# The last two experts' rows kept on chip and added by 0/1 products, pair rows added by GpSimd and TensorE by turns

## What is computed

```python
gate = (softmax(top_v) * pg[:, None])              # two gates a token
h = silu(xb @ w_g[e]) * (xb @ w_u[e])              # D=1024 -> 512
y = (h @ w_d[e]) * wts[:, None]                    # 512 -> 1024
out = zeros_like(xt).at[buf_tok].add(y)            # two rows a token are added
x = layer_norm(ALPHA * x + out, ln3_g, ln3_b)      # ALPHA = 2 ** 0.25
```

## Time and profile before

| | |
|---|---|
| median of 3 runs | 1626.03 us |
| the profiled execution's own time | 1628.42 us |
| its span | 1625.8 us |
| mean granted TensorE clock | 0.978 of full |
| TensorE busy | 1552.3 us (95%) |
| VectorE busy | 1005.0 us (62%) |
| ScalarE busy | 787.0 us (48%) |
| GpSimd busy | 362.8 us (22%) |
| DMA | 352.69 MB, 217 GB/s mean |

### The profile page before, as it was taken

The page is one execution under the profiler, slowest core; times in us unless marked ns, Lnnn a source line. Parts: engine busy times, 40 slices in busy tenths (PEclk is TensorE's granted clock), DMA queues, the critical chain, the costliest instruction groups (busy, mean ns, idle before and its releaser), DMA issues.

```text
span 1625.8 us, 21437 instructions
## 1 busy us (share of the span) xinstructions
PE 1552.3 (95%) x8440; PEld 1279.9 (79%) x8440; DVE 1005.0 (62%) x1282; ACT 787.0 (48%) x1143; POOL 362.8 (22%) x277
## 2 busy tenths in 40 slices
PE   8999999999988999999999988999999999999966
PEld 6877887677766888999777777888888888888842
DVE  5611111777644655222555458989889998999936
ACT  5411121555454013222422234887888887888834
POOL 0000000477862851000122111131111121111005
PEclk9999999999999999999999977999999999999987
DMA  9721111600333545000445536999999999999876
GB/s 356 260 76 39 43 56 59 174 23 19 118 104 132 184 170 193 27 21 1 156 156 175 175 130 251 385 368 396 387 382 399 398 389 393 385 392 398 342 283 282
DMA packets 86331, 352.69 MB, mean 217 GB/s; under 512 B 23512, under 2 KB 28248, under 8 KB 64474
## 3 DMA queue, kind: packets, MB, share of 16 engines
q1 hardware_dynamic: 76106, 331.41, 54.1%
q0 software_dynamic: 9216, 18.89, 3.0%
q10 hardware_dynamic: 912, 1.05, 0.2%
HBM read 321.93 MB, written 43.15 MB: 225 GB/s over the span
## 4 chain that ended last, share of the span: by engine, by line
PE 85%; DVE 5%; DMA 4%; ACT 3%; issue 1%; POOL 0%; SPq 0%; DVEq 0%; POOLq 0%; ACTq 0%
PE M L1348 23%; PE M L1067 12%; PE T L862 6%; PE M L835 6%; PE T L1348 5%; PE T L771 3%; DMA beside<-in_w_exp_up 3%; DVE rounded L1905 3%; PE M L771 3%; PE M L950 2%; PE T L1409 2%; PE T L1139 2%; PE T L1137 2%; PE T L1138 2%; PE M L1171 2%; PE M L1153 2%
## 5 line engine op out<-in xcount | busy, mean ns | idle before, releaser
L1905 DVE TENSOR_TENSOR rounded<-beside,rounded 128x1024 fp32r<-128x1024 f32 (+1 forms) x397 | 471.4, 1233 | 57.2 <-ACT rounded L1791 46.7
L1348 PE MATMUL M<-rounded 128*128 128x512 f32 x1908 | 461.3, 392 | 2.8 <-ACT rounded L1826 1.9
L1348 PEld LDWEIGHTS M<-rounded 128*128 128x128 f32 x1908 | 355.8, 188 | 77.7 <-ACT rounded L1826 2.1
L1791 ACT CAST rounded<-beside 128x1024 fp32r<-128x1024 f32 x256 | 258.9, 1050 | 80.9 <-DMA beside<-in_w_exp_up 75.4
L1067 PE MATMUL M<-rounded 128*128 128x512 f32 x816 | 196.7, 395 | 2.9 <-ACT rounded L1661 1.7
L1067 PEld LDWEIGHTS M<-rounded 128*128 128x128 f32 x816 | 150.1, 188 | 33.9 <-issue 2.0
L1801 ACT CAST rounded<-beside 128x1024 fp32r<-128x1024 f32 x128 | 125.2, 1049 | 24.2 <-DMA beside<-in_w_exp_down 22.3
L2573 POOL DMA_INDIRECT expert_rows<-beside,route_out x32 | 41.8, 1305 | 394.8 <-ACT beside L1832 389.5
L2506 POOL TENSOR_SCALAR arena<-arena,rinv 128x384 f32<-128x384 f32 (+7 forms) x64 | 110.2, 1726 | 48.9 <-DVE rinv L2033 48.7
L1348 PE MATMUL T<-rounded 128*128 128x512 f32 x384 | 108.7, 398 | 0.0
L1905 DVE TENSOR_TENSOR rounded<-T,rounded 128x512 fp32r<-128x512 f32 (+2 forms) x84 | 79.0, 944 | 20.7 <-ACT rounded L1674 17.7
(11 more groups left out here) (374 smaller groups left out, 2462.4 us busy)
## 6 DMA issues: line engine op xcount, KB each, us to landing
beside<-in_w_exp_gate SPq DMA_DIRECT2D x64, 1024.0 KB, 8.1
beside<-in_w_exp_up SPq DMA_DIRECT2D x64, 1024.0 KB, 10.9
beside<-in_w_exp_down SPq DMA_DIRECT2D x32, 2048.0 KB, 11.4
arena<-x_rows SPq DMA_DIRECT2D x27, 512.0 KB, 3.7
x_rows<-arena SPq DMA_DIRECT2D x18, 512.0 KB, 3.1
arena<-expert_rows SPq DMA_DIRECT2D x9, 1024.0 KB, 12.7
arena<-in_x_prompt SPq DMA_DIRECT2D x16, 512.0 KB, 3.9
arena<-in_cache_mem_k SPq DMA_DIRECT2D x8, 1024.0 KB, 5.7
```

Source lines behind the costliest of these rows:

```text
L1348: got = nc.tensor.matmul(out, x[xs], (high, low)[ws](w)[:, c:c + 512], start=(first and n == 0), stop=(last and n == 2))
L1791: nc.scalar.copy(as_both(high(c)), both_raw(c)).then_inc(gu_high, 1)
L1905: return nc.vector.tensor_tensor(out, x, highs.bitcast(f32), ALU.subtract)
```

## The change

1. **Gates in the expert rows.** VectorE computes the gates (divided by ALPHA) before it goes on with the split, multiplies the one-hot matrices `r_hot` with them, and TensorE brings them to slots: 18 plain float32 matmuls of 128x32, ahead of expert 0's transposes. The 20 idle-filling matmuls become 6. `slot_gate` holds a gate for each slot of each expert; ScalarE multiplies by it where it copied before (`results`).
2. **The last two experts stay on chip.** Rows of experts 30 and 31 aren't scattered. ScalarE and VectorE write them as high and low parts over `xT_parts`. GpSimd makes 18 0/1 matrices `hots` (slot by token, one for each expert and tile) in block 28, and TensorE adds the rows by products with them: two parts by two halves, for each expert and tile. The DRAM rows that are never written must read as zero, so SP zeroes all of `expert_rows` (9.4 MB) early.
3. **Pair rows.** Tiles 1, 3, 5 and 7 are added by TensorE with the identity in plain float32 (`pair_rows`), tiles 0, 2, 4, 6 and 8 by GpSimd, two additions a tile (`add_pairs`). VectorE adds `T` to every tile.
4. **Loads.** The x2 rows are loaded in the raw weights' place during the last block, the pair rows while expert 31's gate/up product frees its chunks, once the scatters of experts 28 and 29 have landed.
5. **Last down products.** Expert 31's hidden rows are turned between chunks 1 and 2 of expert 30's down product (`last_two_down`), and the splits on ScalarE and VectorE are reordered to match.
6. **Finish.** Tiles go in the order 0 to 8. Six of them (all but 4, 5 and 6) are finished on VectorE with PSUM operands.

The diff, cut to its core:

```diff
@@ SP, early and in the last block
+            sp.dma_start(ye_dram.rearrange("(p a) (h c) -> p (a h) c", p=P, c=CW),
+                         conv_w[:, 2, :].unsqueeze(1).to_broadcast([P, 4 * NT, CW])).then_inc(pairs_zeroed, 16)
...
+                        for g in (0, 1):
+                            sp.wait_ge(gu_low, 8 * b + 4 * (g + 1))
+                            for t in range(4 * g, 4 * g + 4):
+                                load_x2(t)
...
+            def load_pairs(t):
+                if t < PT:
+                    sp.wait_ge(gu_used, 8 * more + 8 * (NE - 1) + t + 1)
+                else:
+                    sp.wait_ge(down_low, 4 * more + 4 * NE)
+                sp.dma_start(yk[t], ye_pairs[t * P:(t + 1) * P, :, :]).then_inc(last_in[t], 16)
...
-            sp.wait_ge(ye_out[1], 16 * (NE // 2))
-            sp.wait_ge(ye_out[0], 16 * more + 16 * (NE // 2))
+            sp.wait_ge(ye_out[0], 16 * (NE // 2 - 1))
+            load_x2(PT)
+            sp.wait_ge(ye_out[1], 16 * (NE // 2 - 1))
@@ TensorE, before the experts
-            for _ in range(20):
+            for _ in range(6):
                 nc.tensor.matmul(M[0][:, 0:512], sel_slot[:, 0, 0, :], sel_slot[:, 0, 0:4, :], start=True, stop=True)
+            pe.wait_ge(sel_ready, 3)
+            for k in (0, 1):
+                for t in range(NT):
+                    to_slots = sel_slot[:, k, t, :] if t < PT else sel_last[:, k, 0, :]
+                    got = nc.tensor.matmul(T[1][:, 0:NE], to_slots.bitcast(f32), r_hot[:, k, t, :], ...)
+            got.then_inc(rank_ps, 1)
@@ TensorE, the last two experts
+            def last_two_down(b):
+                pe.wait_ge(hidT_high, b)
+                pe.wait_ge(hidT_low, b)
+                pe.wait_ge(ye_rows, b - 1)
+                for k in range(4):
+                    pe.wait_ge(down_low, 4 * b - 4 + k + 1)
+                    x = [hidT_parts[1 - b % 2][s][:, k * P:(k + 1) * P] for s in (0, 1)]
+                    for c in (0, 512):
+                        got = split_product(M[1][:, c:c + 512], x, 8 + k, c, k == 0, k == 3)
+                    got.then_inc(down_used, 1)
+                    if k == 1:
+                        turn_hidden(b, b % 2)
+                last_down(b, b % 2)
@@ TensorE, the finish
+            def rows_of_last(e, t):
+                for part in (0, 1):
+                    for c in (0, 512):
+                        got = nc.tensor.matmul(T[t % 2][:, c:c + 512], hots[e][t], xT_parts[e][part][:, c:c + 512], ...)
+                return got
+
+            def pair_rows(t):
+                pe.wait_ge(last_in[t], ROWS_IN[t])
+                for k in (0, 1):
+                    for c in (0, 512):
+                        nc.tensor.matmul(T[t % 2][:, c:c + 512], ident, yk[t][:, k, c:c + 512], start=(k == 0), stop=False)
@@ ScalarE
-                nc.scalar.copy(yo[u], M[1][:, :]).then_inc(ye_rows, 1)
+                nc.scalar.mul(yo[u], M[1][:, :], gate).then_inc(ye_rows, 1)
...
-                split_down(b, range(4))
+                split_down(b, (0, 1))
                 if not coming:
                     hidden_high(b, u)
+                split_down(b, (2, 3))
@@ VectorE, the finish
+            for p in range(NT):
+                if p - 1 in BY_GAIN:
+                    shift_of(p - 1)
+                if p == PT:
+                    add_shift(p - 2)
+                sum_rows(p)
+                if 0 < p < PT and p - 1 not in BY_GAIN:
+                    scale_shift(p - 1)
+                if p < PT and p - 2 in BY_GAIN:
+                    add_shift(p - 2)
+                if p not in BY_GAIN:
+                    centre_gain(p)
                 add_eps(p)
@@ GpSimd, the finish
+            def add_pairs(t):
+                pool.wait_ge(last_in[t], ROWS_IN[t])
+                nc.gpsimd.tensor_tensor(xl[t], xl[t], yk[t][:, 0, :], ALU.add).then_inc(pool_step, step.next())
+                pool.wait_ge(pool_step, step.value())
+                nc.gpsimd.tensor_tensor(xl[t], xl[t], yk[t][:, 1, :], ALU.add).then_inc(pairs_added, 1)
...
+            add_pairs(BY_POOL[0])
+            for n, t in enumerate(BY_POOL[1:]):
+                add_pairs(t)
+                inverse_deviation(n)
```

More of the change, by code:

```diff
@@ L115, in sem @@
             return ctx.enter_context(nc.semaphore(name))
+        with nc.sbuf_tensor("ident_only", [P, P], f32), nc.sbuf_tensor("hots_at_tables", [P, 6 * P], f32r) as spare:
+            hot_spaces = [spare[:, i * P:(i + 1) * P] for i in range(6)]
         tables = sb("tables", [P, 3 * P + NT * 64 + P + 2 * NT])
@@ L125, in encoder_layer_kernel @@
             x_high = [first[:, :]]
+        with nc.sbuf_tensor("two_rows", [P, 2 * CW], f32), nc.sbuf_tensor("hots_at_conv_w", [P, CW], f32r) as spare:
+            hot_spaces += [spare[:, i * P:(i + 1) * P] for i in range(4)]
         conv_w = sb("conv_w_rows", [P, 3, CW])
@@ L135, in encoder_layer_kernel @@
             x_high.append(second[:, :])
+            hot_spaces += [second[:, i * P:(i + 1) * P] for i in range(8)]
         shift2 = sb("shift2", [P, D])
@@ L787, in _ @@
             for _ in range(3):
[L788 removed]
+                nc.tensor.matmul(M[1][:, 512:], conv_w[:, 2, 0:P], conv_w[:, 2, :], start=True, stop=True)
             pe.wait_ge(mem_in, 32)
@@ L1340, in _ @@
             nc.tensor.matmul(totals, ones, picks[:, PT * NE:], start=False, stop=True).then_inc(rank_ps, 1)
-            for _ in range(20):
+            for _ in range(6):
                 nc.tensor.matmul(M[0][:, 0:512], sel_slot[:, 0, 0, :], sel_slot[:, 0, 0:4, :], start=True, stop=True)
+            pe.wait_ge(sel_ready, 3)
+            for k in (0, 1):
+                for t in range(NT):
+                    to_slots = sel_slot[:, k, t, :] if t < PT else sel_last[:, k, 0, :]
+                    got = nc.tensor.matmul(T[1][:, 0:NE], to_slots.bitcast(f32), r_hot[:, k, t, :], start=(k == 0 and t == 0), stop=(k == 1 and t == PT))
+            got.then_inc(rank_ps, 1)
             def split_product(out, x, w, c, first, last):
@@ L2367, in _ @@
             with dve.If(more > 0):
+                last_low(0)
+                last_low(1).then_inc(ye_rows, 1)
+                dve.wait_ge(ye_rows, NE)
+                dve.wait_ge(hots_ready, NT + 1)
+                nc.vector.memset(patch_tok, -1.0)
+                for u in (0, 1):
+                    dve.wait_ge(ye_out[u], 16 * (NE // 2 - 1))
+                    got = nc.vector.tensor_tensor(yo[u], xT_parts[u][0].bitcast(f32), xT_parts[u][1].bitcast(f32), ALU.add)
+                got.then_inc(more_step, 1)
                 with dve.Fori(0, MORE) as i:
@@ L2575, in scatter, with mark_last_rows @@
                                              oob_is_err=False).then_inc(ye_out[u], 16)
+            def mark_last_rows():
+                for e in (0, 1):
+                    for t in range(NT):
+                        got = nc.gpsimd.tensor_scalar(hots[e][t], iota, patch_tok[:, e, t:t + 1], None, ALU.is_equal)
+                return got
             gather(0, 0)
```

255 lines of the change are left out of this document (142 added, 113 removed).

## The result

The changed kernel takes **1628.96 us** (median of 20 runs, 1625.92 to 1633.09), the kernel before 1625.95 (20 runs, 1622.65 to 1630.48): ratio **1.0019**, 95% interval 1.0012 to 1.0027, so 3.0 us slower. Forecast were 1625.5, 0.5 less than before.

A forecast was written before the change was run, and what follows sets the result against it. TensorE, busy throughout the experts, then a series of waits at the end were taken as the bound. Tail -6.3 and front +5.8 gave -0.5 against the span of 1625.8, carried to the median 1625.5 us; range 1618 to 1632.

The forecast's parts named there:

- Tail, step one: Last experts' down products: with expert 31's transposes moved into expert 30's last product, TensorE ends at 1568.6, gaining 1.8 us.
- Tail, step two: Last down product to first sum: scatter and read-back leave the path, and the first sum starts at 1575.0 us.
- Carried to the median: Whole sum: -0.5 us against the profiled execution's span of 1625.8, taken over to the median of 1626.03, gives 1625.5 us.
- Tail, step three: First sum to the end: last scaling ends 41.2 us after the first sum starts, then 3.3 remain, giving 1619.5.
- The front: Experts' start: first product 4.1 us later, slow clock behind it 2.5, less 0.8 of slack: 5.8 us lost.
- The first rival: Experts' start: clock rises under the six matmuls and stays up, so only 2.0 us are lost, total 1621.7; 20%.
- GpSimd's additions didn't stretch: Finish: the rival claimed additions of 3.0 us beside VectorE instead of 2.36, ending 6 later, total 1631.5; 14%.
- The loop absorbed nothing: Expert loop: the rival claimed it makes up the delay at the experts' start, leaving -6.3 us, total 1619.7; 10%.
- TensorE at 1.2 GHz in the finish: Tail: TensorE's clock falls while it waits between tiles and it paces the finish again, +19.5 us, total 1645; 4%.
- Without cost: Early zeroing, GpSimd's 18 marks and ScalarE's scaling of expert rows by a gate were charged nothing in the sum.
- The fill: Early in the kernel: zeroing 9.4 MB takes 25 us from about 70 on, hidden before input tiles turned at 109.72.
- ScalarE's scaling: Expert loop: rows scaled by a gate rather than copied, up to 0.2 us a block, hidden beside TensorE.

The follow-up runs named there:

- old front: Changed kernel without the 18 narrow matmuls, with 20 idle-filling matmuls again and gates not applied (computation changed): 1621.66 us, 0.9978 of the kernel before.
- turned round: Changed kernel with TensorE's finish products directly behind the last expert's down products and the overflow code behind them: 1627.70 us, 1.0010 of the kernel before.
- code moved back: Kernel with the old front, gates not applied, plus 12 small matmuls for one warm-up matmul at the start of TensorE's program: 1628.81 us, 1.0022 of the kernel before.
- queue in turns: Changed kernel with GpSimd's pair additions split between the powers and tile 8's pair rows added by TensorE: 1624.70 us, 0.9996 of the kernel before.
- both: Changed kernel with TensorE's finish directly behind the last expert, GpSimd's additions split between powers, and tile 8 on TensorE: 1619.56 us, 0.9959 of the kernel before.

## Why the prediction was wrong

One step of the tail failed, and the front cost in most profiles less than a third of what was forecast. Stretches of the kernels with the old and the new finish (us from the last SiLU to the end of the span):

| kernel | tail |
|---|---|
| before, two profiles | 68.9, 66.9 |
| forecast | 62.6 |
| new finish without the pause: old front; turned round, two profiles | 63.2; 63.7, 63.8 |
| changed kernel, two profiles; with ten more matmuls ahead of the jump | 67.3, 68.4; 70.1 |
| old front, code moved back | 68.5 |
| queue in turns, with the pause | 63.4 |
| both; with all tiles on VectorE | 60.6; 58.2 |

- **Tail, step one** held: TensorE stands briefly ahead of a chunk and ends some 1.5 earlier relative to the last SiLU (forecast 1.8). The step left out that the x2 rows are now issued ahead of the last down weights: in six other profiles of the new finish ScalarE stood 1.6 to 2.4 for the DMA of these weights, and the gain was 0.4 to 1.3.
- **Tail, step two is the step that failed.** "TensorE issues 4 rounded products (0.91), the 8 full-f32 instructions ..." left out what stands between them and the last down product, a branch over the overflow code. Before, the same jump lay under the wait for the scatter (that trace has an instruction packet between 1571 and 1572 too) and nothing shows that it cost anything. I asked of each wait that goes what is late next, but only among data and engines, not in TensorE's own instruction stream. The jump cost 2.3 to 2.75, and the clock that fell in it 1.7 more (8.2 from the first row to the first sum, not 6.5): 4.1 in all, 4.5 with the code moved back, of the 6.3. Once, with the queue in turns, the clock did not fall.
- **The base** was wrong by 1 to 2: the profiled tail of 68.9 is the longer of two, and the kernel with the fill alone, whose finish is the old one, has 67.3. "Carried to the median" spread a surplus over the sum that lay in the stretch that the change removes. With the typical tail of 67 the forecast gain is 4.4, not 6.3.
- **Tail, step three** held to 0.2 at each sum, the waits for powers included; turning the queue round gave back 3.4 in the series, where step three charges 3.1 to it, and 3.7 in the times.
- **The front**, forecast 5.8, is 6.3 (4.1 to 8.8) when put alone on the kernel before. In single profiles it is 1.8 seven times of eight, because the clock rose 0.5 to 1.0 us after the start of the narrow matmuls, and 5.4 once, which is the forecast's working: 18 matmuls at 0.50, first product 4 us late. The first rival's condition was nearly met, but its "stays up" failed too: the clock fell as the narrow matmuls ended in all seven. The times don't agree among themselves on the front: with the jump's pause in both, the kernel with the old front (1.0022) is no faster than the changed one (1.0019); without the pause in either, the old front is 5.2 faster (0.9978 against 1.0010). Each of these edits also moves TensorE's code. So what the front costs in the times, and why they say more than most profiles do, stays open.
- **Luck.** By the profiles the tail gave 6.3 less than forecast against its base and the front took some 4 less. The two errors have opposite signs, so the forecast total missed by only 3.5.
- **Rivals.** GpSimd's additions didn't stretch (2.34 to 2.41 each). The loop absorbed nothing. TensorE at 1.2 GHz in the finish did come: behind the pause, as said above, and again for a few microseconds around tile 7 (0.50 in the window 1605.5 to 1608 of the changed kernel), where it cost 1.0 in one execution and nothing in the others, not 19.5.
- **Without cost.** The fill is issued at 70.96 and the third input tile is turned at 111.14, in the earlier trace rows at 109.72; but in this execution the granted clock had been 0.66 from 10 to 20 us, where the kernel before had 0.83, so the delay need not be the fill's. Alone on the kernel before the fill measures 1.1 (-0.8 to 2.9). ScalarE's scaling takes 1.1 beside TensorE, and no wait for it shows.

The sum with what was measured: tail 67.85 less 67.9 (means of two profiles each), 0; middle 571.8 less 570.05, 1.8; ahead of the routing 988.5 less 985.8, 2.7, most of which is the spread of executions, since twelve kernels and profiles with the fill have a mean of 986.9. That gives 1.8 + 1.1 = 2.9, where the times say 3.0. It is a sum that fits, not one that shows its parts.

## What to carry to other kernels

A branch that stood under a wait becomes part of the path when the wait goes. Look for jumps over long code at the place where the path is shortened, put the usual case where the engine falls through to it, and look in the trace for an instruction packet where an engine stands "for issue"; whether it costs anything can change with an edit anywhere ahead of it.

Profile both kernels more than once before a sum of a few microseconds is made against a single execution. The stretches between three or four fixed places tell which part varies.

## What the runs showed of the hardware that I had not expected

- An edit of some 44 instructions in TensorE's first microseconds moved the end of the kernel by 5.3 us in the profile (7.1 in the times). 4.5 of it lie at a jump: a pause of 2.75 us that was not there before, and a granted clock of 0.50 behind it.
- Ten more matmuls ahead of the jump didn't hide it: 2.32 us of pause came behind them, as without them.
- With 36 passes of 128x32 TensorE was busy 8.00 of 8.00 us at a clock of 0.50 in one profile of eight; in the other seven the clock was 1.00 under most of them and 0.50 right behind them. 18 passes of 128x256 took less time in all (2.4 us against 4.4), and the clock behind them was 1.00 in both profiles.
- Behind the same rest of 1.9 us ahead of the last expert the clock was 1.00 in one kernel and 0.50 in another, which came to it 1.5 us later.
